# Gate projections of a hybrid decoder block: thirteen tile pairs instead of twelve by Strassen-like sums, with x loaded a second time for the sums

## The reference

```python
u = rmsnorm(x, g_mix)
proj = u @ w_in       # q, k, v | HGRN2 q, f, i, out-gate | gate_a, gate_b
y_a = stick_breaking_attention(rmsnorm(q), rmsnorm(k), v)        # 8 heads of 128
y_b = rmsnorm(hgrn2_chunkwise(silu(hq), 1 - f, hi, log f)) * silu(og)   # 8 heads of 128
m = sigmoid(gate_a) * (y_a @ p_a) + sigmoid(gate_b) * (y_b @ p_b)
h = x + m @ w_o
out = h + (silu(gate) * val) @ w_down   # gate, val = conv3(rmsnorm(h) @ w_up), 5632 wide each
```

## Time and profile before

| | |
|---|---|
| median of three runs | 2764.08 us |
| the profiled execution, its own time | 2764.32 us |
| its span, first to last instruction | 2762.8 us |
| PE busy | 2757.2 us, 100% |
| DVE, ACT, POOL busy | 2132.9, 1314.0, 427.3 us |
| the plain gate units after the last mix | from 779.8 to 834.5 us |
| the twelve pairs | from 834.5 to 1069.2 us |
| mean granted clock of PE | 1.000 |
| DMA, mean over the span | 149 GB/s |

### The profile page before, as it was taken

How to read it: one execution, slowest core, us unless ns; L and a number is a source line. 1 busy time by engine, 2 the same in 40 slices (tenths; PEclk the granted TensorE clock), 3 DMA queues, 4 the chain that set the end, 5 groups by cost and what they waited for, 6 DMA issues and landing times.

```text
span 2762.8 us, 40001 instructions
## 1 busy us (share of the span) xinstructions
PE 2757.2 (100%) x14150; PEld 2365.8 (86%) x14150; DVE 2132.9 (77%) x3563; ACT 1314.0 (48%) x1807; POOL 427.3 (15%) x579
## 2 busy tenths in 40 slices
PE   9999999999999999999999999999999999999999
PEld 7888888888888888888899988888888888888888
DVE  7776777677778998444568888888888888888884
ACT  5444444444335555333355555555555555555554
POOL 1022153324400000001000111011111101110112
PEclk9999999999999999999999999999999999999999
DMA  5464585666535555444455666666656666665667
GB/s 177 150 179 104 171 209 117 187 185 130 109 122 160 178 170 181 145 136 147 143 169 146 142 143 136 138 138 144 138 135 141 140 138 137 145 137 136 138 144 164
DMA packets 187443, 410.91 MB, mean 149 GB/s; under 512 B 22288, under 2 KB 50320, under 8 KB 186128
## 3 DMA queue, kind: packets, MB, share of 16 engines
q1 hardware_dynamic: 120240, 283.90, 33.0%
q0 software_dynamic: 67040, 124.82, 24.9%
HBM read 347.81 MB, written 112.72 MB: 167 GB/s over the span
## 4 chain that ended last, share of the span: by engine, by line
PE 99%; DVE 0%; DMA 0%; SPq 0%; ACT 0%; issue 0%; DVEq 0%
PE bank L2465 17%; PE bank L2115 12%; PE bank L2117 12%; PE bank L2116 12%; PE bank L2471 9%; PE bank L2562 6%; PE bank L2561 6%; PE bank L2565 6%; PE bank L2353 6%; PE bank L2365 3%; PE bank L2526 2%; PE bank L2528 2%; PE bank L2527 2%; PE bank L2189 1%; PE bank L2179 0%; PE bank L2252 0%
## 5 line engine op out<-in xcount | busy, mean ns | idle before, releaser
L1039 ACT ACTIVATE w_hi<-w_two 128x896 fp32r<-128x896 f32 (+1 forms) x528 | 433.1, 838 | 447.7 <-DVE w_two L1860 407.2
L1867 DVE TENSOR_TENSOR w_lo<-w_two,w_hi 128x896 fp32r<-128x896 f32 (+1 forms) x528 | 496.1, 952 | 85.8 <-ACT w_hi L1039 85.6
L2465 PE MATMUL bank<-v_parts,w_hi 128*128 128x512 f32 x2072 | 503.8, 391 | 0.0
L2465 PEld LDWEIGHTS bank<-v_parts,w_hi 128*128 128x128 f32 x2072 | 379.6, 188 | 72.7
L2115 PE MATMUL bank<-u_both,w_hi 128*128 128x512 f32 x1000 | 393.8, 394 | 0.2 <-DVE w_lo L1207 0.2
L2117 PE MATMUL bank<-u_both,w_lo 128*128 128x512 f32 x1000 | 389.6, 390 | 0.0
L2116 PE MATMUL bank<-u_both,w_hi 128*128 128x512 f32 x1000 | 389.3, 389 | 0.0
L730 POOL DMA_DIRECT2D out_t<-stage x168 | 142.6, 851 | 1159.1 <-ACT stage L1111 1116.0
L1207 DVE TENSOR_TENSOR w_lo<-w_raw,w_hi 128x1024 fp32r<-128x1024 f32 x189 | 230.2, 1221 | 112.2 <-ACT w_hi L748 110.1
L2471 PEld LDWEIGHTS bank<-v_parts,w_lo 128*128 128x128 f32 x2072 | 268.1, 191 | 11.5
L2471 PE MATMUL bank<-v_parts,w_lo 128*128 128x256 f32 x2072 | 271.7, 283 | 0.0
(11 more groups left out here) (314 smaller groups left out, 4885.4 us busy)
## 6 DMA issues: line engine op xcount, KB each, us to landing
w_two<-wslots SPq DMA_DIRECT2D x504, 256.0 KB, 2.7
w_raw<-wstream SPq DMA_DIRECT2D x189, 512.0 KB, 3.5
out_t<-stage POOLq DMA_DIRECT2D x168, 256.0 KB, 4.7
sums_scratch<-wfirst POOLq DMA_DIRECT2D x72, 448.0 KB, 5.7
g_raw<-sums_scratch SPq DMA_DIRECT2D x48, 448.0 KB, 3.4
g_raw<-wgates SPq DMA_DIRECT2D x48, 256.0 KB, 3.2
w_two<-sums_scratch SPq DMA_DIRECT2D x24, 448.0 KB, 3.3
sums_scratch<-sums_scratch POOLq DMA_DIRECT2D x72, 128.0 KB, 4.5
```

Of the source, the lines that this page charges most:

```text
L1039: act.activation(w4_hi[ring][:, 0:width], w4_raw[ring][:, 0:width], ACT.Copy).then_inc(w4_hi_ready, 1)
L1867: dve.tensor_tensor(w4_lo[ring][:, 0:width], w4_raw[ring][:, 0:width], w4_hi[ring][:, 0:width].bitcast(F32), ALU.subtract).then_inc(w4_rea ...
L2465: return nc.tensor.matmul(bank[j].rearrange("p (a c) -> p a c", a=2), w4_hi[ring][:, w * P:(w + 1) * P], both, start=kp == 0, stop=kp == K ...
```

## The change

The first six gate tiles are plain and 26 are in 13 pairs. Four units leave and eight slots come, so `START_P`, where the pairs begin, is behind turn 11. With it go these changes:

- `u_whole` on DVE is gone. ACT's queue issues eight loads of 512 KB of x (`load_x`, in turns 4, 5, 7 and 10) into the sets' places, and ACT scales them in place by the channel's factor (`u_again`, two instructions a set).
- The sets are made one a turn from turn 4 on: set 0 and 1's sums in turn 4, ahead of the last mix, set k + 1 in turn k + 4, set 7 in turn 11. Their places in memory are exchanged so that sets 0, 1 and 2 are free when the last head's `S_hi` is written.
- The weight sums of slots 1 and 3 are also made in memory (`SUMMED`, 54 slots of 104), in batches of 6 with two turns a head on POOL's queue, not batches of 12 with one.
- The last pair's copies stand ahead of the split of the second `y` unit, the first four `y` units use other banks, and their loads wait for later slots.

```diff
-GATE_TILES = 8
+GATE_TILES = 6
-NPRE, NGATE, BATCH = 24, PAIR_SLOTS // 2, 12
+SUMMED = sorted([*range(0, PAIR_SLOTS, 2), 1, 3])
+UNSUMMED = [j for j in range(PAIR_SLOTS) if j not in SUMMED]
+NPRE, NGATE, BATCH = 24, len(SUMMED), 6
-T_UNITS = [5, 6, 8, 10, 11, 12, 14]
+X_LOADS = {4: (0, 1, 2), 5: (3, 4, 5), 7: (6,), 10: (7,)}
+T_FIRST = 4
-    t_at = [R3 + j * 4 * T for j in range(4)] + [32 * 1024, 40 * 1024, tile[0], tile[4]]
+    t_at = [R3 + j * 4 * T for j in (0, 1, 3, 2)] + [40 * 1024, tile[0], 32 * 1024, tile[4]]
-    BANKS2, BANKS3 = [6, 7, 4, 5], [6, 7]
+    BANKS2, BANKS3 = [5, 6, 7, 4], [6, 7]
...
@ SP
-                    sp_.wait_ge(unit_done, START2 + slot + 1)
+                    sp_.wait_ge(unit_done, WSLOTS + START2 - (slot == 1))
@ POOL
-                if turn < HEADS:
-                    pool.wait_ge(unit_done, WSLOTS + turn * HEAD_UNITS + 10)
+                if turn < 2 * HEADS:
+                    pool.wait_ge(unit_done, WSLOTS + turn // 2 * HEAD_UNITS + (3, 10)[turn % 2])
@ ACT
+            def load_x(kp):
+                if kp == 0:
+                    act.wait_ge(S_hi_ready, HEADS)
+                if kp == 3:
+                    act.wait_ge(mix_done, 2 * HEADS)
+                if kp == 6:
+                    act.wait_ge(ssq_done, 3 * HEADS)
+                if kp == 7:
+                    act.wait_ge(yb_ready, HEADS)
+                at_ = 2 * kp * SEQ
+                act.dma_start(u_raw[kp][:, :], x_t[:, at_:at_ + 2 * SEQ]).then_inc(x_arrived[kp], 16)
+
+            def u_again(kp):
+                act.wait_ge(x_arrived[kp], 32)
+                for h in range(2):
+                    here = u_raw[kp][:, h * SEQ:(h + 1) * SEQ]
+                    ins = act.activation(here, here, ACT.Copy, scale=col(par, P_MIX + 2 * kp + h))
+                ins.then_inc(u_raw_ready, 1)
...
                 head_steps(HEADS // HEADS_PER_BODY, -1, HEAD_UNITS + u)
-                if u in T_UNITS:
-                    high_sums(T_UNITS.index(u))
+                k = u - T_FIRST
+                for kp in X_LOADS.get(u, ()):
+                    load_x(kp)
+                if k == 0:
+                    u_again(0)
+                    u_again(1)
+                    high_sums(0)
+                    u_again(2)
+                if 0 <= k < 6:
+                    high_sums(k + 1)
+                if 0 < k < 5:
+                    u_again(k + 2)
+                if k == 6:
+                    u_again(7)
+                if k == 7:
+                    high_sums(7)
...
+                    if j + 1 == PAIR_SLOTS:
+                        gate_copy(GATE_PAIRS - 1)
                     split_ahead(START_P, 0, 0, j)
-                if j % KP == KP - 1 and j // KP < WIDE_PAIRS:
+                if j % KP == KP - 1 and j + 1 < PAIR_SLOTS:
                     gate_copy(j // KP)
-                if j == 3:
-                    high_sums(KP - 1)
@ DVE
-            def u_whole(kp):
...
             for u in range(2 * GATE_TILES):
-                if u in T_UNITS:
-                    kp = T_UNITS.index(u)
-                    u_whole(kp)
-                    if kp > 0:
-                        low_sums(kp - 1)
-                    u_sums(kp)
-                if u == T_UNITS[-1] + 1:
-                    low_sums(KP - 2)
                 if u + LEAD < 2 * GATE_TILES:
                     split_ahead(START_G, 0, 0, u)
-                if u == 2 * GATE_TILES - 2:
-                    gate_sums(1)
                 if u == 2 * GATE_TILES - 1:
                     gate_lo(0)
                 head_steps(HEADS // HEADS_PER_BODY, -1, HEAD_UNITS + u)
                 if u > 0 and u % 2 == 0:
                     gate_tile(u // 2 - 1)
+                k = u - T_FIRST
+                if k == 0:
+                    u_sums(0)
+                if 0 <= k < 7:
+                    low_sums(k)
+                if 0 <= k < 6:
+                    u_sums(k + 1)
+                if k == 7:
+                    u_sums(7)
...
                 if j == 0:
+                    low_sums(KP - 1)
                     gate_tile(GATE_TILES - 1)
-                    u_whole(KP - 1)
-                if j == 2:
-                    u_sums(KP - 1)
-                if j == 4:
-                    low_sums(KP - 1)
@ PE
-                pe.wait_ge(p1_ready, last_copies + 4 + p)
+                pe.wait_ge(p1_ready, last_copies + (2 if p == 2 else 7))
```

More of the change, by code:

```diff
@@ L570, in _ @@
                     sp_.wait_ge(w_ready, START_P + before + 1)
-                if j % 2 == 0:
-                    sp_.dma_start(g_raw[raw][:, :], sums_dram[j // 2, :, :]).then_inc(g_raw_in[raw], 16)
+                if j in SUMMED:
+                    sp_.dma_start(g_raw[raw][:, :], sums_dram[SUMMED.index(j), :, :]).then_inc(g_raw_in[raw], 16)
                 else:
-                    sp_.dma_start(g_raw[raw][:, 0:SC], wgates[j // 2, :, :]).then_inc(g_raw_in[raw], 16)
+                    sp_.dma_start(g_raw[raw][:, 0:SC], wgates[UNSUMMED.index(j), :, :]).then_inc(g_raw_in[raw], 16)
             for slot in range(WSLOTS):
@@ L943, in gate_hi @@
             def gate_hi(j):
-                if j % 2 == 0:
+                if j in SUMMED:
                     act.wait_ge(g_raw_in[raw_place(j)], 16 * raw_loads(j))
                 else:
-                    act.wait_ge(gw_sums, j // 2 + 1)
+                    act.wait_ge(gw_sums, UNSUMMED.index(j) + 1)
                 act.wait_ge(unit_done, WSLOTS + START_P + ((-1, 0, 0)[j] if j < PLACES else j - PLACES + 1))
@@ L971, in y_high @@
                     act.wait_ge(yb_ready, HEADS)
-                act.wait_ge(unit_done, gate_unit(GATE_PAIRS - 2) + c + 1)
+                act.wait_ge(unit_done, gate_unit(GATE_PAIRS - 2) + (1, 2, 4, 4)[c])
                 act.activation(y_hi[:, c * YC:(c + 1) * YC], y_raw[:, c * YC:(c + 1) * YC],
@@ L1645, in gate_sums @@
             def gate_sums(j):
-                w, u = g_raw[raw_place(j)], j // 2
+                w, u = g_raw[raw_place(j)], UNSUMMED.index(j)
                 dve.wait_ge(g_raw_in[raw_place(j)], 16 * raw_loads(j))
@@ L1748, in _ @@
                     wide_step(k)
-                if j + 3 < PAIR_SLOTS and j % 2 == 0 and not first:
+                if j + 3 in UNSUMMED and not first:
                     gate_sums(j + 3)
@@ L2665 @@
         "wstream": weight_stream(w_in[0], p_a[0], p_b[0], w_o[0]),
-        "wgates": np.ascontiguousarray(gates[1::2]),
+        "wgates": np.ascontiguousarray(gates[UNSUMMED]),
         "wslots": wslots,
-        "wfirst": whole_slots(np.concatenate([gates[::2], wslots[:NPRE]])),
+        "wfirst": whole_slots(np.concatenate([gates[SUMMED], wslots[:NPRE]])),
         "params": np.ascontiguousarray(params),
```

## The result

The changed kernel takes 2780.74 us (median of 5 runs, 2779.64 to 2782.27) against 2764.18 us of the kernel before on the same chip (5 runs, 2763.74 to 2764.6): ratio 1.0061, 95% interval 1.0046 to 1.0075. It is slower by 0.6%; the forecast was 2779.6. The profiled run took 2780.74 us by its own time, its span is 2779.2 us, 16.4 more than before.

What follows compares the result with a forecast made beforehand. TensorE bounds, busy 99%, so time is its passes by their pace. Waits 17.85 us, less 2.18 (pair) and 0.4 (copies), give +15.3 on 2764.3: 2779.6 us, 0.55% slower; range 2772 to 2787.

Steps and rivals of the forecast that it cites:

- the loop over two engines: Sets' turns: u waits on ACT and DVE for the turn before; 2 to 2.5 us lost a turn against PE's 5.435.
- The pair: Plain gate tiles: exchanging two (21.74 us) for one pair (19.56 us) saves 2.18 us.
- The turn: Links once around ACT and DVE sum to 7.38 us, 7.98 with a gate tile's product.
- rival (a): Lead covers the loop and turns keep PE's pace: 2761.7 us, not slower; chance 0.10.
- The waits of units 9 to 11: PE waits for late w_lo, at unit 10 behind the tile's product: 1.4, 3.1 and 1.95 us.
- the margin I saw at unit 8: Turn 6: w_lo(8) ready at 789.2, PE wants unit 8 at 791.01, so no wait.
- The first gate slot: g_hi(0) stands behind u_again(7) on ACT, ready at 827.4; PE ready at 819.25, waits 8.15 us.
- The second slot: g_lo(1) ready at 833.1, slot 0 ends at 829.85: PE waits 3.25 us.
- slot 0 at 1.2 GHz: At the low clock it takes 4.9 us, ends 832.3, still ahead of g_lo(1): 0 taken, up to 5.
- Parts at nothing: Sums of slots 1 and 3 in memory, 448 KB loads, last pair's order, ACT's DMA issues: 0 taken, bounds given.
- ACT's own DMA issues: Eight load issues on ACT's queue, 0 to 0.85 us each: 0 taken, up to 3 us.
- The copies' idle of L958: Weight loads of L2353 waited at most 0.8 us for these copies; half taken as gain, 0.4 us.

Runs made afterwards that it cites:

- e5: Changed kernel with each set's rounding one turn later, set 7 behind the first gate slots, g_hi(0) and g_lo(0) ahead of set 6's rounding: 2761.91 us.
- e7: Kernel before (12 pairs, 8 tiles) with only x loaded and scaled on ACT, no u on DVE: 2768.73 us, ratio 1.0017.
- e2: Changed kernel with set 7's scaled copies, sums and rounding moved behind the first gate slots: 2774.86 us, ratio 1.0040.
- e4: Changed kernel with weight sums of slots 1 and 3 on DVE again, those of slots 101 and 103 in memory instead: 2779.93 us.
- e3: Changed kernel with ACT's rounding of each set one turn later, behind the next w_hi: 2767.62 us, ratio 1.0013.
- e6: Changed kernel with u made by DVE, without load_x and u_again, sets 6 and 7 behind the first slots: 2774.92 us.

## Why the prediction was right

The step that carried it was the loop over two engines: not how busy ACT and DVE are (48% and 77% after), but how long one turn takes through both. Point by point:

- **The pair.** Worth 2.18 us. e5, with the waits gone, has a span 2.4 us shorter than the kernel before (2760.4 against 2762.8) and a median 2.16 shorter. By the starts of passes, from the third pass of the first plain gate unit to the first pass of y, it is 327.48 us for 329.73, 2.25 less, with what the copies give in it: right, and all there is. In the changed kernel the pairs behind the first take 19.51 to 19.83 us each, close to the 19.56 forecast.
- **The turn.** Worked out 7.98 us with a tile in it, measured 7.91 and 7.92. The links from rows of other sets held within 0.1: w_lo 1.14, product 0.60, low_sums 1.32, u_sums 1.55, t_hi 0.97, u_again 1.22, w_hi 1.08 with the hand-overs. The turn to 806.21, which has no tile, has the mean square in its place. The prediction names two things that make the loop, u_again ahead of w_hi on ACT and the sums behind w_lo on DVE. In e7 the first is there and the second is not, and the turns take 4.0 to 4.5 us: without the second there is no loss. The set loop of before, which spoke for rival (a), had its sums in the same place as e7 and kept PE's pace as well.
- **The waits of units 9 to 11.** Forecast 1.4, 3.1, 1.95; measured by the starts of passes 1.7, 2.9, 1.7. I had written that the profile would name w_lo three times; unit 10's wait stands under g_out, the tile's product that the timetable had named. Not forecast: 0.5 for sq_lo, since the timetable began 1.6 us too early: the first load of x landed 4.8 us after its issue and not 3.5, and u_again(0) began at 773.14, not at 771.5. That ate the margin I saw at unit 8.
- **The first gate slot.** g_hi began at 827.18 and PE at 828.25, forecast 826.45 and 827.4. The wait is 7.1, not 8.15, because PE was through with unit 11 at 821.0 and not at 819.25, 1.8 us later (0.5 for sq_lo, 0.5 from the start of the program, 0.4 for slower first passes, the rest small differences), and g_hi only 0.7 later. ACT's tail sets when the slot begins; what PE loses ahead of it, it waits less there. So what PE alone loses in the units hardly reaches the total, and that the sum came so near is less proof of each date than it looks.
- **The second slot.** Forecast 3.25. PE reaches the same pass 5.65 us after the first gate pass, where it had taken 2.42: 3.2 more. The profile shows only 1.7 of it as a wait; the other 1.5 are passes at the low clock, which the wait for g_lo(1) would have taken anyway. The prediction had slot 0 at 1.2 GHz end ahead of g_lo(1) all the same, and so took 0 for it; e2 took the cover away: then the low clock costs 1.5 us.
- **Parts at nothing.** Sums of slots 1 and 3 in memory: e4, 0.8 us less than the changed kernel with overlapping ranges of runs, and e5, which keeps them: nothing. ACT's own DMA issues: 0.33 to 0.56 us each, beside its computing. The copies' idle of L958 was put at 0.4 gained; the same idle is 0.5 after for 0.8 before, 0.3.
- **Sum.** Waits by starts of passes 17.5 (forecast 17.85), 0.5 for slower first passes behind them, 0.5 at the start of the program, 0.3 for the copies and 2.18 off: about +16 of the 16.4. The forecast +15.3 was 1.1 low; it had no term for the slower first passes nor for the start, the waits themselves were 0.35 too high. The 0.5 at the start is scatter: the third pass of the first plain gate unit starts at 739.64 before and at 740.11 in the changed kernel, but at 739.51 in e3 and 739.00 in e2, which are the changed kernel up to there. Another 0.2 lies in the feed-forward part, scatter too.

One part stays open: whether e5 is really faster. Its interval goes from 0.9983 to 1.0001.

## What to carry to other kernels

When a value is handed from one engine to the other and back within each turn, add the links once around; if the sum exceeds the turn of the engine that bounds, the excess is lost each turn once the lead is used up, however idle both are. Which links are in the loop is settled by the order on the two queues: with the sums ahead of w_lo a turn with the same work took 4.0 to 4.5 us (e7), behind it 7.9. Letting one side work on what the other made a turn earlier parts the two engines (e3: 13 of 16.6 us back by a single index, the shorter tail included). And move what the next stage's first instruction stands behind on an in-order queue, a late load above all, after it.

## What the runs showed of the hardware

TensorE's granted clock falls to 0.50 (1.2 of 2.4 GHz) even after a wait of 3 us. Busy time by stretch in the changed kernel (from:to, length, PE, PEld, DVE, ACT, POOL, clock, DMA share, GB/s):

```profile
812.00:820.00 8.00, 6.42 (x29) 4.96 (x28) 5.70 (x8) 2.10 (x3) 0.00 (x0) 1.00 0.00 0
820.00:828.00 8.00, 1.18 (x6) 0.64 (x4) 3.86 (x7) 3.12 (x4) 0.54 (x1) 0.77 0.32 98
828.00:831.00 3.00, 2.75 (x9) 2.39 (x10) 2.52 (x5) 0.38 (x2) 0.00 (x0) 0.50 0.25 42
```

The waits of 1.6 and 2.8 us of the units before it, with 5.4 us of passes between, left it at 1.00. Behind the wait of 7.1 us it is 0.50, and passes of L2375 start 0.43 us apart instead of 0.227, until about 831. In e2 the same follows a wait of 3.1 us, and in e7 one of 3.2. In e3 and e6 waits of 1.0 and 2.8 us, and of 0.4 and 2.3 us, close together at the first slots were followed by passes at half rate too, so the length of one wait does not decide it alone. The Trainium skill, "TensorE: Matmul & The Clock Gate", Part 1, has the slow state as the default that activity releases; the runs agree, with 0.50 as the level granted.

The pass that ends a wait is 0.33 us to the next one instead of 0.227, at the full clock too: 799.58 to 799.91 behind the wait for unit 9.

A load issued by ACT costs its queue 0.33 to 0.56 us (line, engine, operation, least/median/most ns, first to last start), and its computing nothing that the timeline shows:

```profile
L974 ACTq DMA_DIRECT2D u_raw<-x_t x8: 334/422/556, 768.3 to 822.2; - x8
...
DMA to landing us min/median/max: 3.6/4.9/7.4
```

The forecast had from POOL's row 0.85 us as its upper end.
